# One-core hybrid trunk: squares of three heads and a scratch clear on POOL, the convolution's mean and centring ahead, norm gaps, dummy matmuls and the opening in another order

## What is computed

```python
for l in range(2):
    mod = silu(c) @ w_mod[l] + b_mod[l]             # 6 vectors of 1024, for latent and for context
    h = rmsnorm(x, g_norm1[l]) * (1 + mod[1]) + mod[0]
    p = split_cols(h @ w_in[l])
    m = mlstm(p[0:5])                               # 4 heads of 64, two directions
    d = diff_attention(p[5:8])                      # 4 heads; rmsnorm of each head's output of 128
    y = conv31(p_a * sigmoid(p_g), w_dw[l]) + b_dw[l]
    c_ = silu(layernorm(y, g_conv_ln[l], b_conv_ln[l]))
    x = x + mod[2] * (concat(m, d, c_) @ w_out[l])
    h = rmsnorm(x, g_norm2[l]) * (1 + mod[4]) + mod[3]
    x = x + mod[5] * (swiglu(h) if l == 0 else top2_of_8_experts(h))
out = rmsnorm(x_latent, g_final)
```

## Time and profile before

| | |
|---|---|
| median of 3 runs | 1466.93 us (1465.52 to 1468.47) |
| the profiled execution, its own time | 1464.65 us |
| its span in the trace | 1462.9 us |
| mean granted clock of PE | 0.973 |
| busy: PE, weight loads, DVE, ACT, POOL | 95%, 78%, 67%, 43%, 12% |
| PE instructions | 7756 |

### The profile page before, as it was taken

How to read it: one execution, slowest core, us unless ns; L and a number is a source line. 1 busy time by engine, 2 the same in 40 slices (tenths; PEclk the granted TensorE clock), 3 DMA queues, 4 the chain that set the end, 5 groups by cost and what they waited for, 6 DMA issues and landing times.

```text
span 1462.9 us, 20612 instructions
## 1 busy us (share of the span) xinstructions
PE 1395.8 (95%) x7756; PEld 1144.4 (78%) x7756; DVE 982.7 (67%) x1476; ACT 632.6 (43%) x997; POOL 181.1 (12%) x134
## 2 busy tenths in 40 slices
PE   7999999989999999999999999898999999999996
PEld 4778787567688888888869887687888888888885
DVE  3755876755744344354469685656898998998896
ACT  3434334652310110010035434635677777777774
POOL 0039970000000000000003960000000000000000
PEclk8999999989999999999999999998999999999998
DMA  9254443322323222222233223149977977977940
GB/s 396 103 201 173 173 173 115 124 108 87 144 91 110 87 103 99 79 109 89 112 116 144 87 87 116 58 150 426 380 289 310 346 305 302 356 291 307 355 171 29
DMA packets 30881, 267.07 MB, mean 183 GB/s; under 512 B 3424, under 2 KB 3552, under 8 KB 4960
## 3 DMA queue, kind: packets, MB, share of 16 engines
q1 hardware_dynamic: 30816, 266.16, 47.7%
HBM read 265.09 MB, written 1.05 MB: 182 GB/s over the span
## 4 chain that ended last, share of the span: by engine, by line
PE 84%; DVE 8%; issue 3%; ACT 3%; DMA 2%; SPq 0%; DVEq 0%; ACTq 0%
PE ps L535 38%; PE ps L989 17%; PE ps L1009 7%; PE ps L852 3%; PE ps L557 3%; PE ps L716 2%; PE ps L752 1%; PE ps L681 1%; PE ps L771 1%; PE ps L542 1%; DMA sb_arena<-mod 1%; DVE sb_egu_lo L2007 1%; PE ps L584 1%; DVE sb_h_lo L1540 1%; PE ps L762 1%
## 5 line engine op out<-in xcount | busy, mean ns | idle before, releaser
L535 PE MATMUL ps<-sb_h_hi,sb_w_hi 128*128 128x512 f32 (+1 forms) x640 | 241.9, 378 | 3.0 <-DVE sb_w_lo L1540 2.7
L535 PE MATMUL ps<-sb_h_hi,sb_w_lo 128*128 128x512 f32 (+1 forms) x640 | 239.5, 374 | 0.0
L535 PE MATMUL ps<-sb_h_lo,sb_w_hi 128*128 128x512 f32 (+1 forms) x640 | 239.4, 374 | 0.0
L989 PE MATMUL ps<-sb_egu_lo,sb_h_lo 128*128 128x512 f32 (+1 forms) x384 | 145.2, 378 | 0.0
L535 PEld LDWEIGHTS ps<-sb_h_hi,sb_w_hi 128*128 128x128 f32 x640 | 121.1, 189 | 28.9 <-DVE sb_w_lo L1540 3.6
L535 PEld LDWEIGHTS ps<-sb_h_hi,sb_w_lo 128*128 128x128 f32 x640 | 121.0, 189 | 21.5
L535 PEld LDWEIGHTS ps<-sb_h_lo,sb_w_hi 128*128 128x128 f32 x640 | 121.2, 189 | 20.7
L1539 DVE CAST sb_w_hi<-sb_arena 128x2048 fp32r<-128x2048 f32 (+1 forms) x38 | 45.5, 1197 | 126.0 <-PE ps L535 114.7
L2007 DVE TENSOR_TENSOR sb_egu_lo<-sb_arena,sb_con_r 128x1024 fp32r<-128x1024 f32 x98 | 115.2, 1216 | 15.3 <-ACT sb_con_r L1360 15.1
L2018 DVE TENSOR_TENSOR sb_ew_lo<-sb_arena,sb_ew_hi 128x1024 fp32r<-128x1024 f32 x88 | 107.1, 1216 | 11.5 <-ACT sb_ew_hi L1373 11.5
L2152 POOL TENSOR_SCALAR sb_arena<-sb_arena,sb_small 128x512 f32<-128x512 f32 (+1 forms) x60 | 104.8, 1746 | 5.9
(11 more groups left out here) (325 smaller groups left out, 3037.2 us busy)
## 6 DMA issues: line engine op xcount, KB each, us to landing
sb_arena<-experts SPq DMA_DIRECT2D x90, 1536.0 KB, 8.8
sb_arena<-mod SPq DMA_DIRECT2D x48, 1024.0 KB, 4.9
sb_arena<-in SPq DMA_DIRECT2D x24, 1024.0 KB, 4.8
sb_arena<-gate SPq DMA_DIRECT2D x11, 1024.0 KB, 4.8
sb_arena<-up SPq DMA_DIRECT2D x11, 1024.0 KB, 4.7
...
```

What stands on the lines that cost most here:

```text
L535: ins = pe.matmul(o, left[a], right[b], start=(k == first and n == 0), stop=(k == final and n == len(PRODUCTS) - 1))
L989: ins = pe.matmul(o, x[:, k, :], w[:, span, :], start=(k == 0 and n == 0), stop=(k == KD - 1 and n == 2))
```

## The change

1. **Opening.** `NORM_AFTER` goes from 3 to 2: the sums of squares follow the third chunk, and the spread of the scale the fourth. The spins behind the first eight chunks are (8, 2, 0, 2, 1, 4, 2, 0) instead of (8, 1, 1, 0, 1, 5, 2, 0). ACT makes the deviation of the norm ahead of the first modulation rows.
2. **Clear.** The clear of 64x3072 goes from DVE to POOL, in both layers, as POOL's first work behind the last tile of the norm; DVE waits for it before "logsig".
3. **Convolution.** PE's mean moves ahead of the first scores, to the end of `project`; DVE's centring moves ahead of the last memory sums. Six spins (layer 0) and five (layer 1) stand ahead of the wait for ACT's squares in `conv_variance`.
4. **Norms (0, 1), (1, 0), (1, 1).** The spread of the scale, with three spins ahead of it, stands right behind the sums of squares; all the modulation chunks of the gap follow. Before, it stood behind the first of them. The spins before the sums of squares of the norm (1, 0) go from 2 to 7.
5. **Gather.** The spins "moe" go from 5 to 12.
6. **Squares of the heads 0 to 2** of each layer go from ACT to POOL; head 3 stays on ACT. PE's sums and DVE's mixing wait for POOL there.

SP's order of loads is the same. The diff:

```diff
--- before.py
+++ after.py
@@ -55,7 +55,7 @@
 TILE = 32
 GROUPS = P // TILE
 FIRST_MOD = 2 * D // CHUNK
-NORM_AFTER = 3
+NORM_AFTER = 2
 LEAD_FIRST = 6
 GATES_FIRST = 3
 VCOLS = 96
@@ -69,10 +69,10 @@
 
 UH = 12
 
-SPIN = {("squares", 0, 0): 0, ("squares", 0, 1): 2, ("squares", 1, 0): 2, ("squares", 1, 1): 0,
+SPIN = {("squares", 0, 0): 0, ("squares", 0, 1): 2, ("squares", 1, 0): 7, ("squares", 1, 1): 0,
         ("norm", 0, 0): 5, ("norm", 0, 1): 4, ("norm", 1, 0): 4, ("norm", 1, 1): 1,
         ("heads", 0): 0, ("heads", 1): 5, ("scores", 0): 5, ("scores", 1): 0, ("conv", 0): 0, ("conv", 1): 0,
-        "router": 8, "moe": 5}
+        ("variance", 0): 6, ("variance", 1): 5, "spread": 3, "router": 8, "moe": 12}
 
 MOD_BATCHES = ([(0, 0, 4), (0, 4, 4)] + [(0, i, 2) for i in range(8, 24, 2)] + [(1, i, 2) for i in range(0, 10, 2)]
                + [(1, 10, 3), (1, 13, 3), (1, 16, 2), (1, 18, 2), (1, 20, 4)])
@@ -81,7 +81,7 @@
 MOD_NORM = {(0, 1): 10, (1, 0): 13, (1, 1): 20}
 MOD_ENDS = ((0, 4), (0, 22), (1, 8), (1, 18))
 MOST = max(MOD_SIZE.values())
-SPIN_FIRST = (8, 1, 1, 0, 1, 5, 2, 0)
+SPIN_FIRST = (8, 2, 0, 2, 1, 4, 2, 0)
 
 MOD_STAGES = {(0, 2 * FIRST_MOD): "modc_first", (0, 48): "modc", (1, 20): "modc_first", (1, 40): "modc",
               (1, 48): "modc_gate"}
@@ -559,15 +559,13 @@
                                         stop=(i == batch(l, first)[-1] and q == KD // GROUPS - 1))
                 ins.then_inc(*pe_done.tick(("mod", l, i)))
 
-            def modulation(l, first, between=None):
+            def modulation(l, first):
 
                 turned = [(x, i) for x, i, _ in MOD_BATCHES if x == l and i < first][-1:]
                 for i in batch(l, first):
                     modulation_chunk(l, first, i)
                     if i == first and turned and turned[0] not in MOD_ENDS:
                         turn_modulation(*turned[0])
-                    if i == first and between:
-                        between()
                 if (l, first) in MOD_ENDS:
                     turn_modulation(l, first)
 
@@ -597,13 +595,16 @@
                                         start=(k == 0), stop=(k > 0))
                 ins.then_inc(*pe_done.tick(("ssq", l, which)))
                 if (l, which) in MOD_NORM:
-                    modulation(1, MOD_NORM[l, which], lambda: norm_spread(l, which))
+                    norm_spread(l, which)
+                    modulation(1, MOD_NORM[l, which])
 
             def norm_spread(l, which):
 
                 lo = low(l) if which else 0
+                o = open_bank(("nscale", l, which))
+                if l + which:
+                    spin(o, SPIN["spread"])
                 pe.wait_ge(*dve_done.at(("ndiag", l, which)))
-                o = open_bank(("nscale", l, which))
                 pe.matmul(o[:, 0:T - lo], ones, rstd[:, 0:T - lo], start=True, stop=True).then_inc(*pe_done.tick(("nscale", l, which)))
 
             def project(l):
@@ -653,6 +654,7 @@
                         if name in LATE_MOD:
                             modulation(0, LATE_MOD[name])
                 memory_sums(l, NH - 1, 1)
+                conv_mean(l)
 
             filler = [[(1, i) for i in MOD_ATTENTION[l]] for l in range(DEPTH)]
 
@@ -773,7 +775,7 @@
                     ins.then_inc(*pe_done.tick(("o", l, h, t)))
 
                 def sum_squares(h):
-                    pe.wait_ge(*act_done.at(("osq", l, h)))
+                    pe.wait_ge(*(pool_done if h < NH - 1 else act_done).at(("osq", l, h)))
                     o = open_bank(("osum", l, h))
                     for b in range(lo // P, NB):
                         ins = pe.matmul(o[:, b:b + 1], kq[:, 2 + h % 2, b * P:(b + 1) * P], ones[:, 0:1],
@@ -784,7 +786,6 @@
                 pe.wait_ge(*dve_done.at(("rope", l, "aq1")))
                 pe.wait_ge(*act_drained.at(("av1", l, NB - 1)))
                 scores(0)
-                conv_mean(l)
                 fill(l, 1)
                 conv_variance(l)
                 memory_turn(l)
@@ -816,8 +817,9 @@
 
             def conv_variance(l):
                 lo = low(l)
+                o = open_bank(("cvar", l))
+                spin(o, SPIN["variance", l])
                 pe.wait_ge(*act_done.at(("csq", l)))
-                o = open_bank(("cvar", l))
                 for b in range(lo // P, NB):
                     for m in range(2):
                         ins = pe.matmul(o[:, b:b + 1], kq[:, m, b * P:(b + 1) * P], ones[:, 0:1], start=(m == 0), stop=(m == 1))
@@ -1292,10 +1294,9 @@
                         h, t = units[n - 2]
                         o = full(("o", l, h, t))
                         f(mix[:, 2 + h, t * P:(t + 1) * P], o[:, 0:P], ACT.Copy).then_inc(*act_drained.tick(("o", l, h, t)))
-                        if t == NB - 1:
+                        if (h, t) == (NH - 1, NB - 1):
                             act.wait_ge(*act_drained.at(("o", l, h, t)))
-                            if h >= 2:
-                                act.wait_ge(*pe_done.at(("osum", l, h - 2)))
+                            act.wait_ge(*pe_done.at(("osum", l, h - 2)))
                             f(kq[:, 2 + h % 2, lo:T], mix[:, 2 + h, lo:T], ACT.Square).then_inc(*act_done.tick(("osq", l, h)))
                     if n in (attention_steps(l) - 6, attention_steps(l) - 4):
                         lead(("out", l, (n + 6 - attention_steps(l)) // 2))
@@ -1422,8 +1423,8 @@
                 ins = f(lam[:, l, 0:2], lam[:, l, 2:4], ACT.Exp)
             ins.then_inc(*act_done.tick("lamexp"))
             squared(0, 0)
+            deviation(0, 0)
             modulation_rows(0, 0)
-            deviation(0, 0)
             lead(("in", 0, IN_ORDER[0]))
             modulation_rows(0, 4)
             for l in range(DEPTH):
@@ -1569,10 +1570,10 @@
                     for name in ("pick", "mask_f", "mask_b"):
                         v.tensor_copy(rounded(name), field(con, CONST, name))
                 v.tensor_copy(ident_r[:, :], ident)
-                settled(v.memset(scratch[0:64, 2 * T:8 * T], 0.0), ("clear", l))
                 split(("in", l, IN_ORDER[1]))
                 split(("in", l, IN_ORDER[2]))
                 dve.wait_ge(*act_done.at(("gln", l)))
+                dve.wait_ge(*pool_done.at(("clear", l)))
                 settled(v.scalar_tensor_tensor(gate_ls[0:R, :], gate_raw[0:R, :], 0.0, gate_ls[0:R, :],
                                                ALU.min, ALU.subtract), ("logsig", l))
                 v.tensor_copy(li[0:NH, :], gate_raw[0:NH, :])
@@ -1738,8 +1739,8 @@
 
             def memory_output(l):
                 t0 = low(l) // P
+                conv_centre(l)
                 memory_sums(l, NH - 1, 1)
-                conv_centre(l)
                 memory_moments(l, NH - 1)
                 maxima(l, 0)
                 dve.wait_ge(*act_done.at(("hstd", l)))
@@ -1796,7 +1797,7 @@
                 def head_mix(h):
                     o = full(("oscale", l, h))
                     dve.wait_ge(*act_drained.at(("o", l, h, NB - 1)))
-                    dve.wait_ge(*act_done.at(("osq", l, h)))
+                    dve.wait_ge(*(pool_done if h < NH - 1 else act_done).at(("osq", l, h)))
                     v.scalar_tensor_tensor(mix[:, 2 + h, lo:T], mix[:, 2 + h, lo:T], stat[:, 0, 0:1], o[:, lo:T],
                                            ALU.mult, ALU.mult).then_inc(*dve_drained.tick(("oscale", l, h)))
                     dve.wait_ge(*dve_drained.at(("oscale", l, h)))
@@ -2135,6 +2136,7 @@
             for l in range(DEPTH):
                 s0 = low(l) // CTX
                 pool.wait_ge(*act_done.at(("h", l, 0, KD - 1)))
+                g.memset(scratch[0:64, 2 * T:8 * T], 0.0).then_inc(*pool_done.tick(("clear", l)))
                 g.memset(upad[:, :, :, 0:PAD], 0.0)
                 g.memset(upad[:, :, :, PAD + SEQ:], 0.0)
                 g.memset(vm_all[:, NB * NH * (DH + 1):], 1.0)
@@ -2153,6 +2155,12 @@
                         pool.wait_ge(*pool_done.at(("product", l, j)))
                         ins = g.tensor_tensor(y, y, p, ALU.add)
                     ins.then_inc(*pool_done.tick(("conv", l) if j == TAPS - 1 else ("tap", l, j)))
+                for h in range(NH - 1):
+                    pool.wait_ge(*act_drained.at(("o", l, h, NB - 1)))
+                    if h >= 2:
+                        pool.wait_ge(*pe_done.at(("osum", l, h - 2)))
+                    o = mix[:, 2 + h, low(l):T]
+                    g.tensor_tensor(kq[:, 2 + h % 2, low(l):T], o, o, ALU.mult).then_inc(*pool_done.tick(("osq", l, h)))
```

## The result

The changed kernel took 1455.41 us in the median of its four executions (1454.82 to 1456.55), the kernel before 1466.22 beside it: a ratio of 0.9925, with a 95% interval of 0.9908 to 0.9942, so 10.8 us less, where 4.6 was forecast. The two profiled executions differ by 1464.65 − 1455.29 = 9.4. The sign was right, and so were most of the places; the size was under half of what came.

What follows compares the result with a forecast made beforehand. PE was taken to bound the kernel, with 84% of the chain, losing time to waits and half clock behind them. The terms summed to 4.6 us off the median of 1466.93, giving 1462.3 us; range 1457.5 to 1470.5.

Steps and rivals of the forecast that it cites:

- Opening: Sums of squares fill PE's 2.06 us wait, so the last modulation chunk starts sooner: +1.5 us (−1.0 to +2.0).
- Clear: Clearing on POOL removes PE's 1.53 us wait for weights split by DVE, layer 0 only: +0.8 us (0.2 to 1.5).
- the half of the hold that was taken off: POOL's 3.0 us clear may hold up DVE: gain 0.2 us if all is lost, 1.5 if none; 0.8 taken.
- Variance, layer 0: Six spins fill PE's 2.96 us wait before the convolution's variance and keep the clock behind it: +2.0 us (0 to 2.5).
- by itself that buys nothing: Earlier convolution mean and centring alone gain nothing, since PE's wait before the variance is for ACT's squares.
- Variance, layer 1: Five spins fill PE's 2.54 us wait; sums and spins behind it run at full clock: +2.4 us (1.0 to 2.9).
- Norms: Reordered spread and spins in three norm gaps: (0, 1) 0, (1, 0) +1.5, (1, 1) −1.3 us.
- Gather: Seven more spins before the experts' gather, only a third covered by a wait, delay it: −2.3 us (−3.4 to −2.2).
- Squares: Head squares moved to POOL take longer but reach PE in time, and ACT is not late: 0 (−0.3 to +1.0).
- A: Rival: half clock follows the filled waits anyway; 1466.5 us at two places (chance 0.22), 1470.7 at all four (0.08).
- B: Rival: POOL's clear is long and holds DVE at the weight split in both layers; up to 1475.5 us, chance 0.06.
- D: Rival: the twelve spins before the gather save the first expert's clock, 2.0 us more, 1460.3 us; chance 0.14.

Runs made afterwards that it cites:

- openback: The changed kernel with the opening order and spins of the kernel before: 1456.67 us, ratio 0.9946 to the kernel before.
- onlyvar: The kernel before with only the six and five spins before the convolution's variance added: 1461.76 us, ratio 0.9985 to the kernel before.

## Why the forecast was right in sign and wrong in size

The mechanism is the one that was forecast: PE's waits are filled, and the work behind them keeps the full clock or loses it for a shorter time. What failed is the size of terms in the sum, above all of the opening and of the clear. Step by step, with the terms as forecast and as the stretches show them:

- *Opening*, +1.5: the stretch is 2.1 to 2.5 us shorter, and it starts some 0.6 earlier. The step that failed is the size: the forecast's own times for the data (35.0 to 35.4 against 37.52) give 2.1 to 2.5 and not "some 2.0", and it took 1.5 of that. It also held the data's times fixed, but the first chunk comes earlier in the changed kernel, and the last chunk's wait ends at 34.38. The order alone is worth 0.7 us by openback's profile and 2.3 at most; why the start moves stays open.
- *Clear*, +0.8: 1.5. The step that failed is the half of the hold that was taken off. Beside the clear only a cast waited, and only one stood there: 1.8 us lost of 3.2 spare.
- *Variance, layer 0*, +2.0: 1.6 to 2.2 at the middle of the profiles, right. But "by itself that buys nothing" was wrong of the early mean: 1.0 us of bank wait hangs on it, and the same term counts 0.78 of that wait as gained.
- *Variance, layer 1*, +2.4: 2.8. No part was lost to DVE's softmax behind.
- *Norms*, 0 + 1.5 − 1.3: (0, 1) loses 0.7 in most profiles; (1, 0) gains 1.4 in most; (1, 1) costs 0.9 where the old order kept its clock and gains 0.5 where it didn't.
- *Gather*, −2.3: −1.75, outside the term's range. The price of a spin was too high. 2.40 us is the length of a row of ten records, which holds the end of the last; in a run a spin takes 5.27 / 12 = 0.44.
- *Squares*, 0: 0.

With the middle of the opening (1.5, plus 0.6), 1.5, 1.9, 2.8, −0.7, 1.4, −0.2 and −1.75 this adds to 7.1 of the 9.5 us; the rest isn't assigned to a place. Some of it is chance in the one profile of the kernel before: from the start of the last scatter matmul to the end of the span, which the change does not touch, it takes 13.9 us, onlyvar 13.1 and the changed kernel 13.1 to 13.4. Opening, clear and variance of layer 1 share one slip: a bound was in hand from a row, and the value taken was shaved from it. The 10.8 us of the first executions contain 1.3 us of chance against the 9.5 of all.

The rivals. A came in part, not at its price: with the waits filled, half clock still stood in the opening in all 15 profiles of the changed kernel and its variants, though mostly for 3 us instead of 10, and behind the variance of layer 0 in 8 of 13. There the stretch is 9.38 to 11.33 us, and 8.67 or 8.68 in the five others; in the kernel before it is 11.55. So these places gained although half clock was still there. A's premise, that half clock begins only at or behind single-column sums, does not hold: it stands behind the memory sums (842 to 846 us above), and in the kernel before it began while PE still waited for ACT's squares in layer 1, ahead of the sums at 904.92 (columns as in the earlier trace rows):

```profile
903.00:904.90 1.90, 0.00 (x0) 0.00 (x0) 0.41 (x1) 1.89 (x4) 0.00 (x0) 0.71 1.00 414
```

B did not come, at 2.81 us. D did not, since the half clock of the first expert stayed (996 to 999 us), and it could not have paid, since DVE bounds the first expert: its 2.0 us was a price of PE's time in a stretch where PE isn't the bound.
